# Gate one-hots in two scaled float16 parts in place of three bfloat16 parts

## What is computed

```python
expert = i1 * N_SUBKEYS + i2
gate = jax.nn.softmax(best_v, axis=-1).astype(h.dtype)
...
u = jnp.take(u_tab, ex, axis=0)
act = jax.nn.gelu(jnp.einsum('thkd,td->thk', u, hx), approximate=False) * gx
vv = jnp.take(v_tab, ex, axis=0)
return jnp.einsum('thk,thkd->td', act, vv)
```

## Time and profile before

| what | us |
|---|---|
| median of 3 runs | 2172.35 |
| lowest, highest run | 2169.05, 2172.98 |
| span of the profiled execution, first to last instruction | 2164.7 |
| PE busy | 2097.8 (97%) |
| PEld busy | 1894.7 (88%) |
| DVE busy | 1574.3 (73%) |
| ACT busy | 1049.4 (48%) |
| POOL busy | 378.4 (17%) |

### The profile page before, as it was taken

The page is one execution under the profiler, slowest core; times in us unless marked ns, Lnnn a source line. Parts: engine busy times, 40 slices in busy tenths (PEclk is TensorE's granted clock), DMA queues, the critical chain, the costliest instruction groups (busy, mean ns, idle before and its releaser), DMA issues.

```text
span 2164.7 us, 50057 instructions
## 1 busy us (share of the span) xinstructions
PE 2097.8 (97%) x19768; PEld 1894.7 (88%) x19768; DVE 1574.3 (73%) x2866; ACT 1049.4 (48%) x1801; POOL 378.4 (17%) x182
## 2 busy tenths in 40 slices
PE   8999999999999999999899999999999999999997
PEld 7888999999888988888688889999998889888885
DVE  6655897788788559955576558958887784698555
ACT  5544445444544444455455444454444554444443
POOL 0022699100000000000001236990000000000000
PEclk9999999999999999999999999999999999999998
DMA  6212355444444554455342134454444445444551
GB/s 265 94 46 100 135 177 191 158 154 149 168 170 173 194 175 149 161 194 194 131 144 96 43 122 146 180 182 151 153 156 169 167 170 197 170 150 162 193 194 67
DMA packets 46619, 335.07 MB, mean 155 GB/s; under 512 B 5168, under 2 KB 5296, under 8 KB 6320
## 3 DMA queue, kind: packets, MB, share of 16 engines
q1 hardware_dynamic: 46512, 333.61, 43.0%
HBM read 332.54 MB, written 1.05 MB: 154 GB/s over the span
## 4 chain that ended last, share of the span: by engine, by line
PE 85%; issue 5%; POOL 4%; DVE 4%; ACT 1%; DMA 1%; POOLq 0%; SPq 0%; ACTq 0%
PE PS L1650 33%; PE PS L1621 28%; PE PS L1295 9%; PE PS L1639 4%; POOL low L433 3%; PE PS L1311 3%; PE PS L1488 1%; PE PS L1521 1%; PE PS L1635 1%; PE PS L1532 1%; DMA ring<-in_w_slabs 1%; ACT high L457 1%; PE PS L1343 1%; PE PS L1394 0%; DVE low L796 0%
## 5 line engine op out<-in xcount | busy, mean ns | idle before, releaser
L648 ACT CAST high<-ring 128x1024 fp32r<-128x1024 f32 x512 | 535.9, 1048 | 553.1 <-PE PS L1621 435.6
L1621 PE MATMUL PS<-hTh,high 128*128 128x256 f32 x2048 | 588.5, 287 | 9.2 <-ACT GA L652 3.4
L1621 PE MATMUL PS<-hTl,high 128*128 128x256 f32 x2048 | 577.3, 282 | 0.0
L1621 PE MATMUL PS<-hTh,low 128*128 128x256 f32 x2048 | 577.0, 282 | 0.0
L1061 DVE TENSOR_TENSOR low<-ring,high 128x1024 fp32r<-128x1024 f32 x416 | 506.7, 1219 | 26.3 <-ACT high L648 18.1
L1621 PEld LDWEIGHTS PS<-hTh,high 128*128 128x128 f32 x2048 | 385.9, 188 | 13.8 <-issue 6.7
L1621 PEld LDWEIGHTS PS<-hTl,high 128*128 128x128 f32 x2048 | 386.1, 189 | 1.3
L1621 PEld LDWEIGHTS PS<-hTh,low 128*128 128x128 f32 x2048 | 385.8, 188 | 0.0
L1650 PE MATMUL PS<-high,WH 128*128 128x512 f32 x1024 | 322.6, 396 | 0.0
L1650 PE MATMUL PS<-low,WH 128*128 128x512 f32 x1024 | 316.2, 390 | 0.0
L1650 PE MATMUL PS<-high,WL 128*128 128x512 f32 x1024 | 315.4, 389 | 0.0
(11 more groups left out here) (258 smaller groups left out, 2931.6 us busy)
## 6 DMA issues: line engine op xcount, KB each, us to landing
ring<-in_peer_slabs SPq DMA_DIRECT2D x256, 1024.0 KB, 4.8
ring<-in_w_slabs SPq DMA_DIRECT2D x58, 1024.0 KB, 4.8
xres<-in_x SPq DMA_DIRECT2D x2, 512.0 KB, 4.4
out<-obuf SPq DMA_DIRECT2D x2, 512.0 KB, 2.6
cst<-in_consts SPq DMA_DIRECT2D x1, 680.0 KB, 10.2
praw<-in_p_t SPq DMA_DIRECT2D x1, 512.0 KB, 14.9
gfin<-in_g_final SPq DMA_DIRECT2D x1, 512.0 KB, 5.7
vec<-in_vecs SPq DMA_DIRECT2D x1, 356.0 KB, 7.1
```

The source lines that it names most:

```text
L648: act.copy(high[:, (c0[L] + j) % DEEP], ring[:, place, half * D:(half + 1) * D]).then_inc(part_hi, 1)
L1621: ins = mm(PS[:, 6 + j % 2, 0:SEQ], u[:, b, ks], h[:, k], start=n == 0, stop=n == 3 * KT - 1)
```

## The change

The gate is multiplied by 2^15 when ACT copies it out of PSUM. It is then split into two float16 parts: its rounding to float16, and the rest rounded to float16. All one-hots, the iota and the repeats are float16. The multiplication of the gates into `GA` takes a factor 2^-15 as well: `scalar_tensor_tensor` with an immediate in place of `tensor_tensor`. In chunks 0 and 2 a token takes two products in place of three. In chunk 1 it takes one product of 64 columns in place of two; `sum_gates` adds the halves as it did.

```diff
-        hot2 = place("hot2", R + 22528, [2, 3, GROUP, WIDEST], BF16)
+        hot2 = place("hot2", R + 22528, [2, 2, GROUP, WIDEST], F16)
...
-                    act.copy(repeats[:, b], decoded[:, :, tokens].unsqueeze(3).broadcast_to([P, 5, GROUP, REP])).then_inc(repeated, 1)
+                    act.copy(repeats[:, b], decoded[:, :, tokens].unsqueeze(3).broadcast_to([P, 4, GROUP, REP])).then_inc(repeated, 1)
...
-                        act.copy(gate_T[:], PS[:, 5, 0:SEQ]).then_inc(slot_T, 1)
+                        act.activation(gate_T[:], PS[:, 5, 0:SEQ], ACT.Identity, scale=GATE_UP).then_inc(slot_T, 1)
...
                 link(dve.tensor_copy(decoded[:, 2], gate_T[:]))
-                link(dve.tensor_tensor(gate_rest[:], gate_T[:], decoded[:, 2], ALU.subtract))
-                link(dve.tensor_copy(decoded[:, 3], gate_rest[:]))
-                dve.tensor_tensor(decoded[:, 4], gate_rest[:], decoded[:, 3], ALU.subtract).then_inc(parts_made, 1)
+                dve.tensor_tensor(decoded[:, 3], gate_T[:], decoded[:, 2], ALU.subtract).then_inc(parts_made, 1)
...
-                                      is_i2[:, b, :, 0:width].rearrange("p t (a c) -> p t a c", c=REP).unsqueeze(1).broadcast_to([P, 3, GROUP, width // REP, REP]),
-                                      repeats[:, b, 2:5].unsqueeze(3).broadcast_to([P, 3, GROUP, width // REP, REP]), ALU.mult).then_inc(hots_made, 1)
+                                      is_i2[:, b, :, 0:width].rearrange("p t (a c) -> p t a c", c=REP).unsqueeze(1).broadcast_to([P, 2, GROUP, width // REP, REP]),
+                                      repeats[:, b, 2:4].unsqueeze(3).broadcast_to([P, 2, GROUP, width // REP, REP]), ALU.mult).then_inc(hots_made, 1)
...
-                        dve.tensor_tensor(acts, acts, gate_sum[:], ALU.mult).then_inc(gated, 1)
+                        dve.scalar_tensor_tensor(acts, acts, 1 / GATE_UP, gate_sum[:], ALU.mult, ALU.mult).then_inc(gated, 1)
...
-                        dve.tensor_tensor(acts, acts, PS[:, 4 + b, 0:GROUP * width].rearrange("p (t i) -> p i t", t=GROUP), ALU.mult).then_inc(gated, 1)
+                        dve.scalar_tensor_tensor(acts, acts, 1 / GATE_UP, PS[:, 4 + b, 0:GROUP * width].rearrange("p (t i) -> p i t", t=GROUP), ALU.mult, ALU.mult).then_inc(gated, 1)
...
-                            mm(PS[:, 4 + b, at:at + 2 * width], hot1[:, b, t], hot2[:, b, 0:2, t, 0:width], start=True, stop=False, skip_group_check=True)
-                            ins = mm(PS[:, 4 + b, at + width:at + 2 * width], hot1[:, b, t], hot2[:, b, 2, t, 0:width], start=False, stop=True, skip_group_check=True)
+                            ins = mm(PS[:, 4 + b, at:at + 2 * width], hot1[:, b, t], hot2[:, b, :, t, 0:width], start=True, stop=True)
                             continue
-                        for part in range(3):
-                            ins = mm(PS[:, 4 + b, t * width:(t + 1) * width], hot1[:, b, t], hot2[:, b, part, t, 0:width], start=part == 0, stop=part == 2)
+                        for part in range(2):
+                            ins = mm(PS[:, 4 + b, t * width:(t + 1) * width], hot1[:, b, t], hot2[:, b, part, t, 0:width], start=part == 0, stop=part == 1)
```

More of the change, by code:

```diff
@@ L9 @@
 F32R = mybir.dt.float32r
-BF16 = mybir.dt.bfloat16
+F16 = mybir.dt.float16
 U32 = mybir.dt.uint32
@@ L42 @@
 REP = 8
+GATE_UP = 2.0 ** 15
 A_EXP, A_TOP, A_LOOP = 32, 44, 48
@@ L162, in hybrid_encoder @@
         zeros = place("zeros", R + 25088, [P])
-        iota_half = place("iota_half", R + 25216, [NSUB], BF16)
+        iota_half = place("iota_half", R + 25216, [NSUB], F16)
         praw = place("praw", R + 24064, [DEPTH, 2, SEQ])
@@ L213, in hybrid_encoder @@
         WL = place("WL", R + 20992, [2, SEQ], F32R)
-        hot1 = place("hot1", R + 21504, [2, GROUP, NSUB], BF16)
-        hot2 = place("hot2", R + 22528, [2, 3, GROUP, WIDEST], BF16)
[L216 to L219, removed]
+        hot1 = place("hot1", R + 21504, [2, GROUP, NSUB], F16)
+        hot2 = place("hot2", R + 22528, [2, 2, GROUP, WIDEST], F16)
+        is_i2 = place("is_i2", R + 23680, [2, GROUP, WIDEST], F16)
+        decoded = place("decoded", R + 24064, [4, SEQ], F16)
+        repeats = place("repeats", R + 24704, [2, 4, GROUP, REP], F16)
         gate_T = place("gate_T", R + 19968, [SEQ])
```

## The result

| | before | after |
|---|---|---|
| median | 2170.7 us (4 runs, 2167.53 to 2172.98) | 2133.65 us (4 runs, 2132.01 to 2135.72) |
| ratio to before | | 0.9829, 95% interval 0.9816 to 0.9842 |
| span of the profiled execution | 2164.7 us | 2131.3 us |

The changed kernel is 1.7% faster, 37 us. The forecast was 2133.1 us, worked out from the median of the three runs before that were known then, 2172.35.

What follows compares the result with a forecast made beforehand. PE was taken to set the pace: 26.4 us in the first and last stages plus 13.1 us in the middle, less 0.3 us for late VectorE, took 39.2 us off the 2172.35 us median, giving 2133.1 us, range 2129.5 to 2141.

Steps and rivals of the forecast that it cites:

- PE sets the pace in all three stages: First, middle and last stage of each layer: PE waits for nobody, so its removed products all count, 39.5 us.
- The price of a product, outer stages: First and last stage: eight of 24 products fewer per spread, 0.207 us a spread, 128 spreads, 26.4 us off PE.
- The narrow product: Middle stage: eight 32-column products fewer per spread, 0.0255 us each, 64 spreads, 13.1 us; bounds 9.2 and 15.4.
- VectorE in the last stage: Last stage: VectorE's step 3.275 us against PE's 3.233 uses up a 1.13 us lead, costing 0.3 us for both layers.
- The gate instruction costs nothing more: Gate multiplication on VectorE: scalar_tensor_tensor with an immediate takes as long as tensor_tensor; the other bound was 0.06 us more.
- the half-rate rival: Gate instruction on VectorE runs at half rate, 0.40 us more, giving 2159 to 2165 us; chance 0.03.
- The rival float16: One-hots on VectorE go slower in float16 than in bfloat16, 84 us more, 2256 us or part of it; chance 0.05.
- The 7.65 us around the span: Whole execution: the span lies 7.65 us below the median of the runs, and this difference was let stand.

## Why the prediction was right

**PE sets the pace in all three stages.** Right, and shown from both sides: with PE's products cut alone, the first two stages are as short as in the changed kernel; with VectorE's work cut alone, nothing moves.

**The price of a product, outer stages: 0.0258 us, 26.4 us in all.** The sum fitted, its two halves did not quite. First stage: steps 0.21 us shorter, as put, and the loop's branch gave 0.9 us a layer on top, which I had not seen although the trace of before shows it (six steps of 3.71 us among those of 3.55). Last stage: 0.173 a step in place of 0.207, because each spend became 0.03 us longer. Together that is 2 x (7.25 + 5.37) = 25.2 us over the 124 steps of the two stages in two layers; the price put gives 25.7. That the two misses, each near 2 us in all, went opposite ways is luck; neither was in the sum.

**The narrow product: 0.0255 us, 13.1 us in all.** Measured 0.026 and 13.2. The nearest row (48 columns) was the better guide than the chain's own division of a pair. By the rule of the Trainium skill that the prediction names ("TensorE: Matmul & The Clock Gate", section "Wait — 56ns, not 53.3ns?") a 64-column product starts an estimated 29.2 ns after the one before. The trace agrees: 29 to 30 ns, all but the 39 at the head of a spread.

**VectorE in the last stage: 3.275 us against PE's 3.233, 0.3 us lost at the end.** VectorE took 3.276. The lead at the start was put at 1.13 us and was 1.17. The 0.3 us did not come, and the lead at the end was 0.91 us and not near zero, since PE itself took 3.267. That is the same term as above: PE's step was put 0.034 us too short. The room that VectorE had left came from this miss.

**The gate instruction costs nothing more.** Right, by L848's row; the half-rate rival is refuted by the rows of the gate itself.

**The rival float16.** Refuted: hot1 takes 681 ns, as against 685 before, and bfloat16 in its place changes no step.

**The 7.65 us around the span.** This step was wrong and did no harm. The span of every run of the changed kernel is 1.8 us below its time (2133.12 and 2131.3), and so is that of each run of the kernel before that was made beside the experiments. By that the profiled execution of before took about 2166.5 us and was one of its quick ones. The rest of the 7.65 us does not lie around the span: it is a difference from one execution to the next, of the kind that the mixing stage's window shows. I had subtracted the gain from the median, so the end stayed right; a forecast of the span, 2125.5, was 5.8 us off.

**How close the number is.** From the first spread to the last spend the two layers gain 38.9 us where 39.2 was put; the medians differ by 37.05. That the forecast hit the median within 0.6 us is in part luck, since the median of before alone fell by 1.65 us with one more run.

## What to carry to other kernels

Where two engines are both full, compare their paces over many steps and read the lead of the one that is behind: here it told to a step or two when VectorE would take over. Shorten such an engine together with the other; either cut alone would have brought 0 or 28 us in place of 37. Count products, not columns, where a product is short: here one of 32 or 48 columns gave back 25 to 26 ns, and one of 64 takes 29.

## What was not expected

- A loop's branch on PE costs about 0.15 us when 24 short products stand right ahead of it and nothing when a run of long ones does. Rotating the loop gave 1.8 us by the steps, 0.08%, for no change in the work; the ratio of the runs, 0.9985, has 0.9975 to 0.9995 as its interval.
- A spend of 12 long products took 2.82 us behind a spread of 24 short ones and 2.85 behind 20, 16 or 8, with VectorE busy or not; one step in which VectorE came just late had 2.82 behind 16.
- A per-partition scalar in place of an immediate adds 0.06 us to a VectorE instruction of 256 (480 against 417 ns) and of 384 elements (614 against 550): a fixed price.
